# Orders at the borders of the stages of a hybrid decoder layer: later modulation tiles, other rings for the last groups, other places for gelus and early transfers

## What is computed

```
mod = silu(c) @ w_mod + b_mod                       # 6 x 2048 values: sh1, sc1, g1, sh2, sc2, g2
h = rms_norm(x, norm_mix) * (1 + sc1) + sh1
z = h @ w_in                                        # 42 chunks of 128 columns
ya = rg_lru(conv(xa)) * gelu(ga)                    # 6 blocks
yb = dilated_attention(qb, kb, vb, rel_bias)        # 6 heads, a T5 bias by distance
yc = stick_breaking_attention(qc, kc, vc)           # 4 heads
x = x + g1 * (concat(rms_norm(ya), rms_norm(yb), rms_norm(yc)) @ w_out)
h = rms_norm(x, norm_ffn) * (1 + sc2) + sh2
ids, g = top16 of product keys of (h @ wq)          # 8 heads
x = x + g2 * sum_k g[k] * gelu(h . u_tab[ids[k]]) * v_tab[ids[k]]
out = rms_norm(x, final_norm)
```

## Time and profile before

| | us |
|---|---|
| median of 3 runs (2133.51 to 2137.69) | 2134.61 |
| the profiled execution, its own time | 2135.38 |
| its span | 2133.6 |
| TensorE busy in it | 2069.0 (97%) |
| VectorE busy | 1383.8 (65%) |
| ScalarE busy | 742.7 (35%) |
| mean granted TensorE clock | 0.988 of full speed |

### The profile page before, as it was taken

The page is one execution under the profiler, slowest core; times in us unless marked ns, Lnnn a source line. Parts: engine busy times, 40 slices in busy tenths (PEclk is TensorE's granted clock), DMA queues, the critical chain, the costliest instruction groups (busy, mean ns, idle before and its releaser), DMA issues.

```text
span 2133.6 us, 31064 instructions
## 1 busy us (share of the span) xinstructions
PE 2069.0 (97%) x12256; PEld 1861.9 (87%) x12256; DVE 1383.8 (65%) x1840; ACT 742.7 (35%) x791; POOL 16.1 (1%) x30
## 2 busy tenths in 40 slices
PE   7999997999999998999999999999999999999997
PEld 5888886779988998999999999999999999999786
DVE  6675776747788986565555655555656555555697
ACT  2014112436312344334344343343443433433333
POOL 0000000000000000000000000000000000000000
PEclk8999999999999999999999999999999999999999
DMA  9999888645443657555565555554655556545894
GB/s 389 421 418 373 281 343 361 232 145 196 163 153 118 218 217 290 193 208 203 176 223 192 191 204 190 209 207 174 221 192 196 203 185 215 202 178 215 335 410 137
DMA packets 99209, 500.34 MB, mean 235 GB/s; under 512 B 8416, under 2 KB 41488, under 8 KB 42960
## 3 DMA queue, kind: packets, MB, share of 16 engines
q1 hardware_dynamic: 81840, 362.27, 46.0%
q10 hardware_dynamic: 13680, 112.20, 14.2%
q0 software_dynamic: 3632, 25.06, 3.0%
HBM read 477.32 MB, written 22.18 MB: 234 GB/s over the span
## 4 chain that ended last, share of the span: by engine, by line
PE 89%; DMA 7%; DVE 3%; issue 1%; ACT 1%; ACTq 0%; SPq 0%; DVEq 0%
PE ps L506 16%; PE ps L495 11%; PE ps L497 11%; PE ps L496 11%; PE ps L786 5%; PE ps L787 5%; PE ps L788 5%; PE ps L799 5%; PE ps L797 5%; PE ps L798 5%; DMA mod_first<-wmod 5%; PE ps L743 3%; PE ps L645 1%; PE ps L647 1%; PE ps L646 1%
## 5 line engine op out<-in xcount | busy, mean ns | idle before, releaser
L497 PE MATMUL ps<-h_hi,wlo 128*128 128x256 f32 x1952 | 553.6, 284 | 0.0
L495 PE MATMUL ps<-h_hi,whi 128*128 128x256 f32 x1728 | 490.3, 284 | 5.4 <-ACT act_u L1074 5.4
L496 PE MATMUL ps<-h_lo,whi 128*128 128x256 f32 x1728 | 490.2, 284 | 0.0
L1573 DVE TENSOR_TENSOR yacc<-yacc,ps 128x512 f32<-128x512 f32 x208 | 143.1, 688 | 368.0 <-PE ps L799 368.0
L497 PEld LDWEIGHTS ps<-h_hi,wlo 128*128 128x128 f32 x1952 | 375.7, 192 | 0.0
L1539 DVE TENSOR_TENSOR vlo<-vraw,vhi 128x2048 fp32r<-128x2048 f32 x116 | 260.7, 2288 | 137.9 <-ACT vhi L1120 137.9
L495 PEld LDWEIGHTS ps<-h_hi,whi 128*128 128x128 f32 x1728 | 332.9, 193 | 7.6 <-issue 5.6
L496 PEld LDWEIGHTS ps<-h_lo,whi 128*128 128x128 f32 x1728 | 332.9, 193 | 2.0
L1096 ACT ACTIVATE whi<-wraw 128x2048 fp32r<-128x2048 f32 x120 | 228.9, 1914 | 148.7 <-DMA wraw<-wst 146.1
L1535 DVE TENSOR_TENSOR wlo<-wraw,whi 128x2048 fp32r<-128x2048 f32 x120 | 269.4, 2284 | 16.6 <-ACT whi L1096 16.6
L1074 ACT ACTIVATE act_u<-ps 128x256 f32 (+1 forms) x128 | 49.0, 383 | 639.2 <-PE ps L497 576.3
(11 more groups left out here) (269 smaller groups left out, 2664.2 us busy)
## 6 DMA issues: line engine op xcount, KB each, us to landing
vraw<-vtab SPq DMA_DIRECT2D x116, 1024.0 KB, 6.8
wraw<-wst SPq DMA_DIRECT2D x111, 1024.0 KB, 4.8
wraw<-wst ACTq DMA_DIRECT2D x91, 1024.0 KB, 5.5
mod_ring<-wmod SPq DMA_DIRECT2D x58, 1024.0 KB, 11.3
mod_first<-wmod SPq DMA_DIRECT2D x22, 1024.0 KB, 20.2
gates_dram<-gstage ACTq DMA_DIRECT2D x4, 4096.0 KB, 16.9
gring<-gates_dram SPq DMA_DIRECT2D x64, 256.0 KB, 5.1
g_ring<-wmod POOLq DMA_DIRECT2D x16, 1024.0 KB, 9.5
```

Of the source, the lines that this page charges most:

```text
L495: mm(dst, hi, src_hi, start=first, stop=False)
L496: mm(dst, hi, src_lo, start=False, stop=False)
L497: return mm(dst, lo, src_hi, start=False, stop=last)
```

## The change

Six edits, none of which adds or removes arithmetic:

1. The T5 bias: POOL writes `rel_rows` out only when 15 slabs are multiplied, ACT waits for that write before it copies values to the place behind them, and VectorE adds the bar to `relbias` just ahead of the attention's logits. `lw` and `mix_sb` change places with modulation tiles in SP's queue.
2. VectorE at the start: the first two modulation tiles come before the first root, the first coefficients after a quarter of `hid` and not after all four, and the decay polynomial after all 32 tiles.
3. `M_MID` is 36 and not 44, and ACT asks for the next weights between its roundings of y.
4. The last three steps of the output projection go step by step for the first token half, and together only for the second.
5. The first gelus of the split blocks stand ahead of the roundings that wait for weights.
6. The last groups take their V tiles from rings in the order V, W, W, V and not V, V, W, W, with other places of the `gring` loads. The loops on SP and ACT are written out.

More of the change, by code:

```diff
@@ L79 @@
 TAILS = LAG // GB // 4
-V_TAIL = NV - 4 * TAILS + 2
-N_TAIL = V_TAIL - 2
+N_TAIL = NV - 4 * TAILS
 G2_FROM = N_TAIL + 1
@@ L1249, in part_done, with h_lower @@
                                 ALU.add).then_inc(s_modv, 1)
+            dve.wait_ge(s_rel, 32)
[14 more added lines that the diff above has]
+                                pcol("norm_mix", kk, 1), ALU.add, ALU.mult).then_inc(s_coef, 1)
+            def h_lower(hi):
+                for kk in range(KD):
+                    dve.wait_ge(s_hhi, kk + 1)
+                    V.tensor_tensor(h_lo[:, kk, :], h32[:, kk, :], hi[:, kk, :].bitcast(F32),
+                                    ALU.subtract).then_inc(s_h, 1)
             dve.wait_ge(s_lam, 1)
```

64 lines of the change are left out of this document (17 added, 47 removed).

## The result

The changed kernel took 2113.52 us (median of 4 runs, 2111.27 to 2120.07), the kernel before 2135.24 beside it: a ratio of 0.9902 with a 95% interval of 0.9878 to 0.9927. It is faster, as forecast, but by 22 us and not by 39, and lies above the range of 2090 to 2110. Its profiled execution took 2113.12 us with a span of 2111.3, 22.3 less than before's 2133.6.

What follows compares the result with a forecast made beforehand. TensorE, busy 97% of the span, was taken as the bound, with DMA binding the first stage. Savings of 4.9 + 13.1 + 5.6 + 6.5 + 8.9 = 39.0 us from 2135.38 gave 2096 us, range 2090 to 2110.

Steps and rivals of the forecast that it cites:

- Edit 1 and 2, the start: First stage: moving the bias's transfers out of full DMA saves 4.9 us; the earlier TensorE start helps cover it.
- Edit 3, the start of the projection: Output projection's start: `out_lo(0)` no longer stands behind six waiting tiles; sums of squares start 13.1 us earlier.
- Edit 3 and 4, its end: Projection's end: products of steps 13 and 14 cover step 15's weights, and VectorE covers the moved tiles; 5.6 us saved.
- only 0.55 busy there: Output projection's steps: DMA share given as reason that tiles between `out_lo` steps would not wait; that slower case had 0.02.
- the `x1` rows are asked for behind the last of these tiles: Output projection: the x1 rows' request comes about 20 us ahead of their use.
- the term of 5.6: Projection's end: ACT's tiles of h start at 471.9 and not 477.47, 5.6 us earlier.
- the middle gives less: Rival, output projection: a new wait (squares, x1 or first half's weights) takes half of 18.7 us; 2105 us, chance 0.12.
- Edit 5: Split blocks: block 23 starts when block 22 ends, then block 24 waits for `w_lo`; 6.5 us saved.
- Edit 6: Last groups: earlier tiles for group 53 save 6.1 us and earlier `gring` requests 3.0, less 0.2: 8.9 us.
- no wait for `gring` would be left: Last groups: gates requested two groups ahead remove the waits for `gring`, 3.0 us.
- Bytes bind the last groups: Rival, last groups: full DMA makes g2 or V tiles late; tail 5.9 down to 4, 2099 to 2101 us, chance 0.22.
- The clock falls in one of the short gaps: Rival: a remaining gap of 1.9 or 2.3 us draws TensorE's lower clock, costing 3.0 us; 2099 us, chance 0.08.

Runs made afterwards that it cites:

- run 10: Changed kernel with POOL writing the bias's rows early again, among the first 16 slabs: 2116.73 us.
- run 9: Changed kernel with `M_MID` back at 44, so the eight tiles stand ahead of the output projection again: 2118.54 us.
- run 5: Changed kernel with x1 rows requested ahead of the fifth tile between the projection's steps and subkeys at the first quarter of x1: 2106.32 us.
- run 6: run 5 with the projection's last three steps again taken together for both token halves: 2113.35 us.
- run 11: run 3 with the split blocks' gelus behind the roundings again: 2117.48 us.
- run 3: Changed kernel with VectorE adding group 0's quarters of y1 ahead of the work for group 1: 2107.72 us.
- Run 1: Changed kernel with group 53's gates requested ahead of the last block's wait and group 54's 2 MB of V tiles: 2105.12 us.
- run 8: Changed kernel with the edits of Run 1, run 3 and run 5, and step 4's weights rounded before y's second six roundings: 2097.47 us.

## Why the prediction was wrong, point by point

**Edit 1 and 2, the start: right.** 3.9 of 4.9 in the changed kernel, and 4.2 to 5.8 in the eleven profiles made from it that keep edit 1. The transfer of the bias was the cause (run 10). The write starts at 136.94 us, when the fifteenth slab is multiplied, and not at about 131.

**Edit 3, the start of the projection: right.** The sums of squares come 13.3 us nearer to the last slab, and 15.7 later without the edit (run 9).

**Edit 3 and 4, its end: this step failed.** The prediction costed the eight tiles against VectorE (4.45 us of 5.44 in a step) and called the DMA engines "only 0.55 busy there", with the row of before. But the edit itself doubles that: a second megabyte a step makes 385 GB/s of 420. And "the `x1` rows are asked for behind the last of these tiles, about 20 us ahead of their use" counted when they are needed, and not whom they delay: they stand for 16.7 us in full engines, together with the subkeys, which the prediction did not speak of. Put elsewhere (run 5) the stretch is 102.03, 5.4 less than before's 107.43 and what the term of 5.6 says. That it agrees is partly luck: edit 4 by itself is worth 7.6 (run 6 against run 5), as it also removes the half clock behind the gap, and a part of that is taken back, by the lower clock that run 5 drew behind step 4's gap and by the tiles, which cost at most 2.3 (run 9 against run 5). The rival "the middle gives less" named x1 and half the gain; that was its mechanism, with 6.5 us (18.7 less the 12.2 seen) in place of 9.

**Edit 5: the size was off, since a wait took its place.** It is worth 5.4 us (run 11 against run 3; 6.5 predicted), by one profile of each. In the changed kernel 3.1 are seen, because group 0's y1 then waits 2.8 us for VectorE. The prediction followed the weights as far as block 24 and stopped there; one row on, the V tiles of group 1 are asked for at 795, behind the same weights, and VectorE's queue holds `add_y(0)` behind them.

**Edit 6: the larger half failed.** "The cause: group 53's tiles go into a V buffer that group 51 frees" was true of before, and the tiles did come early. But a group needs its gates as well, and the new order asks for those of group 53 behind 2 MB for group 54. A stall of 6.1 us stayed, with another transfer as its end. That it kept its length to a tenth (27.91 and 27.88 us for two groups) is chance: the gap is 3.2 us in place of 4.0, and where the clock did not fall behind it the two groups took 24.9 to 25.6. Run 1 removes it with one request moved. That no wait for `gring` would be left held for TensorE's 3.0 us in this profile, of which 0.4 are left. In six others it did not hold: TensorE waited 1.6 or 1.7 us in the last groups in three and 4.8 to 5.8 in three.

**The rivals.** "Bytes bind the last groups" is not the cause of the missing 5.9, since runs 1 and 8 win it at the same 410 GB/s; it is probably what makes the gates late at the end in some runs, since the DMA engines are full up to 2060 us. "The clock falls in one of the short gaps" occurred at step 4, where the lower clock cost 1.6 us in place of the 3.0 that the prediction put on it, and at the gap of group 53, which the prediction wanted gone.

With the three causes and step 4's weights mended, run 8 gives 2097.5 us, where 2096 was predicted: the waits that the prediction wanted gone could go; the change had put other requests in front of them. That the number is met so closely is partly luck, since the prediction had left step 4's gap in place.

## What to carry to other kernels

When work that brings its own transfers moves into a quiet stretch, add its bytes to those that are there and compare with the full rate: a share of 0.55 leaves room for less than as much again. For each request that moves, list what then stands behind it in the same queue, and everything that stood at its end. And when one wait is removed, work out for the same instruction when its other operands land: the stall can stay under another name.
